# First projection of a transformer kernel: five of eight weight jobs as three products of short-fp32 parts, parameter loads on the GpSimd queue

## The reference, cut to what matters

```python
h = rms_norm(x, norm1_g[l]) * (1 + sc1) + sh1
z = h @ w_in[l]                       # 256 x 1024 by 1024 x 3896
y_fox = fox_mixer(z[..., :FOX_COLS], ...)
y_rwkv = rwkv7_mixer(z[..., FOX_COLS:], ...)

def fox_mixer(zf, qn_g, kn_g, on_g, forget_b):
    q, k, v, g, f_logit, a_k, a_v = split_cols(zf, FOX_SPLITS)
    k = a_k * shift_prev(k) + (1 - a_k) * k      # a_k, a_v: sigmoids
    v = a_v * shift_prev(v) + (1 - a_v) * v
    q = rms_norm(q, qn_g)
    k = rms_norm(k, kn_g)
    log_f = jax.nn.log_sigmoid(f_logit + forget_b)
    cum = jnp.cumsum(log_f, axis=1)
    ...                                          # attention of 8 heads of 64

def rwkv7_mixer(zr, mu, ...):
    zr = zr + mu * (shift_prev(zr) - zr)         # all 1824 columns
    r, k, v, wd, ad, gd = split_cols(zr, RWKV_SPLITS)
    ...
```

## Time and profile before

| | us |
|---|---|
| median of 3 runs | 1384.34 (1383.09 to 1384.56) |
| profiled execution, whole | 1383.96 |
| span in the profile | 1381.5 |
| PE busy | 1313.4 (95%) |
| DVE busy | 622.7 (45%) |
| ACT busy | 351.2 (25%) |
| POOL busy | 44.1 (3%) |

### The profile page before, as it was taken

The page is one execution under the profiler, slowest core; times in us unless marked ns, Lnnn a source line. Parts: engine busy times, 40 slices in busy tenths (PEclk is TensorE's granted clock), DMA queues, the critical chain, the costliest instruction groups (busy, mean ns, idle before and its releaser), DMA issues.

```text
span 1381.5 us, 19977 instructions
## 1 busy us (share of the span) xinstructions
PE 1313.4 (95%) x7904; PEld 834.0 (60%) x7904; DVE 622.7 (45%) x1174; ACT 351.2 (25%) x609; POOL 44.1 (3%) x50
## 2 busy tenths in 40 slices
PE   5999998999899999999999999899999998999997
PEld 2545546965544444544444444578778566999985
DVE  2135377567422222222222222565448743677753
ACT  0202320012122221222222121454321112344542
POOL 0014200000000000000000000300000000000000
PEclk9999999999999999999999999999889999999998
DMA  9684284049299999999999996654611131455551
GB/s 342 235 263 152 101 366 160 2 117 407 112 397 422 419 409 423 412 418 418 417 414 421 407 419 240 230 166 153 135 19 61 62 122 61 153 183 185 186 197 73
DMA packets 96072, 341.19 MB, mean 247 GB/s; under 512 B 9248, under 2 KB 42680, under 8 KB 67213
## 3 DMA queue, kind: packets, MB, share of 16 engines
q1 hardware_dynamic: 85728, 321.16, 60.6%
q10 hardware_dynamic: 8109, 12.33, 3.4%
q0 software_dynamic: 2176, 6.86, 1.5%
HBM read 333.22 MB, written 1.05 MB: 242 GB/s over the span
## 4 chain that ended last, share of the span: by engine, by line
PE 86%; DVE 7%; DMA 4%; issue 1%; ACT 1%; ACTq 0%; DVEq 0%
PE bank L1890 17%; PE bank L1364 12%; PE bank L1906 9%; PE bank L1379 6%; PE bank L1380 6%; PE bank L1381 6%; PE bank L1852 3%; PE bank L1870 2%; PE bank L1872 2%; PE bank L1853 2%; DMA small<-in_norm_g 2%; PE bank L1350 2%; PE bank L1391 2%; PE bank L2280 2%; DMA ring<-in_w_in 1%; PE bank L1978 1%
## 5 line engine op out<-in xcount | busy, mean ns | idle before, releaser
L1364 PE MATMUL bank<-ring,xT 128*128 128x512 f32 (+1 forms) x416 | 180.4, 590 | 6.2 <-DVE xT L2454 2.3
L1364 PEld LDWEIGHTS bank<-ring,xT 128*128 128x128 f32 x416 | 79.5, 194 | 94.6 <-issue 84.3
L1906 PE MATMUL bank<-dn,tmp 128*64 128x512 f32 x528 | 120.6, 598 | 0.0
L3008 DVE TENSOR_TENSOR xT<-bank,mod 128x512 fp32r<-128x512 f32 x66 | 45.7, 692 | 157.9 <-ACT mod L1114 150.6
L3001 DVE SCALAR_TENSOR_TENSOR tmp<-silu_c,rc,bank 128x256 f32<-128x256 f32 x33 | 22.6, 685 | 196.8 <-ACT silu_c L1101 191.4
L1379 PE MATMUL bank<-mod,w_high 128*128 128x256 f32 x304 | 85.1, 280 | 0.0
L1380 PE MATMUL bank<-xn,w_high 128*128 128x256 f32 x304 | 85.1, 280 | 0.0
L1381 PE MATMUL bank<-mod,ring 128*128 128x256 f32 x304 | 84.8, 279 | 0.0
L3495 DVE TENSOR_TENSOR ring<-ring,w_high 128x1024 fp32r<-128x1024 f32 x60 | 70.7, 1221 | 21.7 <-ACT w_high L1299 20.2
L1906 PEld LDWEIGHTS bank<-dn,tmp 128*64 128x64 f32 x528 | 35.0, 136 | 68.3 <-issue 68.3
L1114 ACT ACTIVATE mod<-bank 128x512 fp32r<-128x512 f32 x64 | 38.2, 597 | 133.8 <-PE bank L1906 133.8
(11 more groups left out here) (654 smaller groups left out, 2296.9 us busy)
## 6 DMA issues: line engine op xcount, KB each, us to landing
dn<-in_exp_w_down SPq DMA_DIRECT2D x66, 1024.0 KB, 10.6
ring<-in_exp_w_gate SPq DMA_DIRECT2D x34, 1024.0 KB, 9.9
ring<-in_exp_w_up SPq DMA_DIRECT2D x34, 1024.0 KB, 12.5
gu_odd<-in_exp_w_gate SPq DMA_DIRECT2D x32, 1024.0 KB, 10.3
gu_odd<-in_exp_w_up SPq DMA_DIRECT2D x32, 1024.0 KB, 12.3
ring<-in_w_ffn_in SPq DMA_DIRECT2D x22, 1024.0 KB, 5.1
ring<-in_w_in SPq DMA_DIRECT2D x7, 2048.0 KB, 11.3
ring<-in_w_in SPq DMA_DIRECT2D x14, 912.0 KB, 4.9
```

The costliest lines, as they stand in the source:

```text
L1364: mm = pe.matmul(bank[lin_bank(o)][:, 0:n], lhs(k, t), ring[:, j % RING, k * n:(k + 1) * n], start=(k == 0), stop=(k == kt - 1 and not bias))
L1906: mm = pe.matmul(bank[6 + h][CHUNKS[c], :], act_eT[:, 0, k, CHUNKS[c]], dn[:, 2 * parity + c, lo:lo + BANK], start=(k == 0), stop=(k == D_ ...
L3008: dve.tensor_tensor(y_low[:, c], bank[6 + h][:, :], y_high[:, c].bitcast(F32), ALU.subtract)\
```

## The change

- J_K, J_V, J_Q, J_R and J_KR (`SPLIT`) are computed by `split_job` as three products each: 48 matmuls instead of 16. J_LORA, J_VR and J_G stay as they are.
- ScalarE makes the high parts of the weights (`split_high`, from `ring` into the new `w_high_1`, one buffer of two halves), VectorE the low ones in place of the weights (`split_low`), in pieces of 1024 columns, four a job. The parts of `xT` are made once, in two halves (`xT_high_1` by ScalarE, `xT_low_1` by VectorE).
- A split job is loaded as two halves of 1 MB. Half 0 of a load waits for the first half of job j-2 (`in_done`), half 1 for its end. `split_high` of half 0 waits until both halves have landed and the first half of the job before is used; that of half 1 waits for the last matmul of the job before, and stands behind its two copies (`copies_beside_split`). TensorE takes half 0 for both tiles, then half 1 for both.
- The loads of `forget_b`, `fxp`, `mu`, of the ten constants and matrices, and of `rwp` and `gain` move to POOL's queue; the ten wait for the end of J_LORA, `rwp` and `gain` for the first lerp and the end of J_Q. `ada_b`'s rows stay with ScalarE.
- The shift of J_LORA moves ahead, right behind the forget gate's chain on ScalarE.
- VectorE's low parts stand between its other steps. Later counts of the shared semaphores are offset accordingly; the diff leaves these lines out, but for one.

```diff
--- before.py
+++ after.py
@@ -259,6 +259,8 @@
+with ExitStack() as before_aug:
+    w_high_1 = stack_r(before_aug, "w_high_1", [P, 2, KT // 2 * BANK])
@@ -581,14 +583,20 @@
-def job(kind, w, lo, n, kt=KT, bias=None, more=0):
+def job(kind, w, lo, n, kt=KT, bias=None, more=0, halves=False):
+    def half(h):
+        ks = slice(h * kt // 2, (h + 1) * kt // 2)
+        dst = lambda slot: ring[:, slot, 0:kt * n].rearrange("p (k n) -> p k n", k=kt)[:, ks, :]
+        return dst, A[w].rearrange("(k p) n -> p k n", p=P)[:, ks, lo:lo + n]
...
-    parts = [part(0, lo, n - more)]
+    parts = [half(0), half(1)] if halves else [part(0, lo, n - more)]
     if more:
@@ -601,9 +609,12 @@
 J_LORA, J_K, J_V, J_Q, J_R, J_KR, J_VR, J_G = range(len(IN_JOBS))
+SPLIT = (J_K, J_V, J_Q, J_R, J_KR)
 for j, (lo, n) in enumerate(IN_JOBS):
...
         job("in", "w_in", lo, n + FG, more=FG)
+    elif j in SPLIT:
+        job("in", "w_in", lo, n, halves=True)
     else:
@@ -661,6 +672,29 @@
+HALF = KT // 2 * BANK
+xT_high_1 = mod_12[:, 0:2, :].rearrange("p a (k c) -> p (a k) c", c=T * P)
+xT_low_1 = xn_low[:, :, :].rearrange("p a (k c) -> p (a k) c", c=T * P)
+def landed_of(j):
+    return sum(16 * len(jobs[i][4]) for i in range(j % RING, j + 1, RING))
+def split_piece(a, j, half, q):
+    lo = half * HALF + q * PIECE
+    return a[:, j % RING, lo:lo + PIECE]
+def high_piece(half, q):
+    return w_high_1[:, half, q * PIECE:(q + 1) * PIECE]
+def piece_no(j, half, q):
+    return 4 * SPLIT.index(j) + 2 * half + q + 1
+IN_1 = 4 * len(SPLIT)
@@ -747,6 +781,15 @@
         for j in range(first, last):
+            if j in SPLIT:
+                for h, (dst, src) in enumerate(jobs[j][4]):
+                    if j >= RING:
+                        if h == 0 and j - RING in SPLIT:
+                            sp.wait_ge(in_done, SPLIT.index(j - RING) + 1)
+                        else:
+                            sp.wait_ge(lin_mm, last_of(j - RING))
+                    sp.dma_start(dst(j % RING), src).then_inc(w_full[j % RING], 16)
+                continue
             if j >= RING:
...
@@ -907,13 +950,22 @@
     rstd(small[:, 18:20], small[:, 16:18])
-    act.wait_ge(ada_mm, 1)
-    act.dma_start(forget_b[:, :], bcast(A["fox_forget_b"])).then_inc(forget_loaded, 16)
-    for j in range(RING):
-        act.wait_ge(w_full[j], 16 * len(jobs[j][4]))
-    for i, name in enumerate(("fox_qn_g", "fox_kn_g", "fox_on_g")):
-        act.dma_start(fxp[:, i, :], bcast(A[name])).then_inc(forget_loaded, 16)
-    act.dma_start(mu[:, :], bcast(A["rw_mu"])).then_inc(mu_loaded, 16)
+    for h in range(2):
+        c = slice(h * KT // 2, (h + 1) * KT // 2)
+        act.wait_ge(h_ready, (h + 1) * KT // 2)
+        act.activation(xT_high_1[:, c, :], xT[:, c, :], ACT.Copy).then_inc(x_high_made, 1)
+    def split_high(j, half):
+        s = SPLIT.index(j)
+        if half == 0:
+            act.wait_ge(w_full[j % RING], landed_of(j))
+            if s:
+                act.wait_ge(in_done, s)
+        elif s:
+            act.wait_ge(lin_mm, last_of(SPLIT[s - 1]))
+        for q in range(2):
+            act.activation(high_piece(half, q), split_piece(ring, j, half, q), ACT.Copy).then_inc(in_high_made, 1)
@@ -935,7 +987,10 @@
-    for t in range(T):
+    split_high(J_K, 0)
+    for t in range(T):
+        if t:
+            split_high(J_K, 1)
         act.wait_ge(lin_mm, after(J_LORA, t))
@@ -948,30 +1003,25 @@
     act.activation(fs[:, 4, 0:16], fs[:, 3, 0:16], ACT.Ln, bias=1.0).then_inc(fox_ln, 1)
-    for t in range(T):
-        in_copy(J_K, t)
-    for name in CONST_1:
-        act.dma_start(cst[name][:, :], consts[name]).then_inc(par_loaded, 16)
-    act.dma_start(lora_up[0:DECAY_R, :], A["rw_decay_up"]).then_inc(par_loaded, 16)
-    act.dma_start(lora_up[DECAY_R:P, :], A["rw_iclr_up"]).then_inc(par_loaded, 16)
-    act.dma_start(gate_up[:, 0, :], A["rw_gate_up"][0:P, :]).then_inc(par_loaded, 16)
-    act.dma_start(gate_up[0:GATE_R - P, 1, :], A["rw_gate_up"][P:GATE_R, :]).then_inc(par_loaded, 16)
+    shift_group(0, J_LORA)
+    def copies_beside_split(j, following):
+        split_high(following, 0)
+        for t in range(T):
+            in_copy(j, t)
+        split_high(following, 1)
+    copies_beside_split(J_K, J_V)
     for b in range(2):
...
             .then_inc(ada_rows, 16)
-    for t in range(T):
-        in_copy(J_V, t)
+    copies_beside_split(J_V, J_Q)
     act.wait_ge(lin_evac, after(J_V, 1))
     shift_rows(kv_prev, z_fox[:, :, 512:1536], kv_shifted)
-    for i, name in enumerate(("rw_w0", "rw_a0", "rw_k_k", "rw_k_a", "rw_r_k", "rw_lnx_g", "rw_lnx_b")):
-        act.dma_start(rwp[:, i, :], bcast(A[name])).then_inc(par_loaded, 16)
-    act.dma_start(gain[:, 1, :], bcast(A["norm2_g"])).then_inc(gain_loaded[1], 16)
-    shift_group(0, J_LORA)
-    for t in range(T):
-        in_copy(J_Q, t)
-    for t in range(T):
-        in_copy(J_R, t)
+    copies_beside_split(J_Q, J_R)
+    copies_beside_split(J_R, J_KR)
     shift_group(1, J_R)
@@ -1440,15 +1490,37 @@
     keep_warm(4, 7)
+    def split_job(j):
+        full[j % RING] += 16 * len(jobs[j][4])
+        for half in range(2):
+            for t in range(T):
+                o = outputs[(j, t)]
+                if half == 0 and o >= 2:
+                    pe.wait_ge(lin_evac, o - 1)
+                for i in range(KT // 2):
+                    k = half * KT // 2 + i
+                    if t == 0 and i % 2 == 0:
+                        pe.wait_ge(in_low_made, piece_no(j, half, i // 2))
+                    mm = product(bank[lin_bank(o)][:, :],
+                                 [a[:, k, t * P:(t + 1) * P] for a in (xT_high_1, xT_low_1)],
+                                 [w_high_1[:, half, i * BANK:(i + 1) * BANK],
+                                  w_low[:, j % RING, k * BANK:(k + 1) * BANK]], k == 0, k == KT - 1)
+                if half:
+                    mm.then_inc(lin_mm, 1)
+            if half == 0:
+                mm.then_inc(in_done, 1)
     dense(J_LORA, first_lhs)
-    dense(J_K, xTk)
+    pe.wait_ge(x_low_made, 2)
+    split_job(J_K)
     pe.wait_ge(logf_ready, 1)
...
     for j in (J_V, J_Q, J_R, J_KR):
-        dense(j, xTk)
+        split_job(j)
     keep_warm(10, 2)
...
@@ -1993,7 +2065,7 @@
                 if t == 0 and i % 2 == 0:
-                    pe.wait_ge(in_low_made, (u - 2) * PIECES + i // 2 + 1)
+                    pe.wait_ge(in_low_made, IN_1 + (u - 2) * PIECES + i // 2 + 1)
                 mm = product(b, [a[:, k, t * P:(t + 1) * P] for a in (xT_high, xT_low)],
...
@@ -2343,6 +2415,20 @@
+    pool.wait_ge(ada_mm, 1)
+    pool.dma_start(forget_b[:, :], bcast(A["fox_forget_b"])).then_inc(forget_loaded, 16)
+    for j in range(RING):
+        pool.wait_ge(w_full[j], 16 * len(jobs[j][4]))
+    for i, name in enumerate(("fox_qn_g", "fox_kn_g", "fox_on_g")):
+        pool.dma_start(fxp[:, i, :], bcast(A[name])).then_inc(forget_loaded, 16)
+    pool.dma_start(mu[:, :], bcast(A["rw_mu"])).then_inc(mu_loaded, 16)
+    pool.wait_ge(lin_mm, after(J_LORA, 1))
+    for name in CONST_1:
+        pool.dma_start(cst[name][:, :], consts[name]).then_inc(par_loaded, 16)
+    pool.dma_start(lora_up[0:DECAY_R, :], A["rw_decay_up"]).then_inc(par_loaded, 16)
+    pool.dma_start(lora_up[DECAY_R:P, :], A["rw_iclr_up"]).then_inc(par_loaded, 16)
+    pool.dma_start(gate_up[:, 0, :], A["rw_gate_up"][0:P, :]).then_inc(par_loaded, 16)
+    pool.dma_start(gate_up[0:GATE_R - P, 1, :], A["rw_gate_up"][P:GATE_R, :]).then_inc(par_loaded, 16)
     pool.wait_ge(mu_loaded, 16)
@@ -2355,6 +2441,11 @@
         pool.sem_inc(lerp_done, 1)
+        if i == 0:
+            pool.wait_ge(lin_mm, after(J_Q, 1))
+            for r, name in enumerate(("rw_w0", "rw_a0", "rw_k_k", "rw_k_a", "rw_r_k", "rw_lnx_g", "rw_lnx_b")):
+                pool.dma_start(rwp[:, r, :], bcast(A[name])).then_inc(par_loaded, 16)
+            pool.dma_start(gain[:, 1, :], bcast(A["norm2_g"])).then_inc(gain_loaded[1], 16)
     pool.wait_ge(experts_copied, 1)
@@ -2453,7 +2544,22 @@
             .then_inc(h_ready, 1)
+    for h in range(2):
+        c = slice(h * KT // 2, (h + 1) * KT // 2)
+        dve.wait_ge(x_high_made, h + 1)
+        dve.tensor_tensor(xT_low_1[:, c, :], xT[:, c, :], xT_high_1[:, c, :].bitcast(F32), ALU.subtract)\
+            .then_inc(x_low_made, 1)
     link(dve.memset(kv_prev[0:1, 0, :], 0.0))
+    def split_low(j, half):
+        for q in range(2):
+            dve.wait_ge(in_high_made, piece_no(j, half, q))
+            dve.tensor_tensor(split_piece(w_low, j, half, q), split_piece(ring, j, half, q),
+                              high_piece(half, q).bitcast(F32), ALU.subtract).then_inc(in_low_made, 1)
+    split_low(J_K, 0)
+    split_low(J_K, 1)
@@ -2463,20 +2569,30 @@
     dve.tensor_tensor(fs[:, 5, 0:16], fs[:, 1, 0:16], fs[:, 4, 0:16], ALU.subtract).then_inc(logf_ready, 1)
+    split_low(J_V, 0)
     dve.wait_ge(sc_mm, SC_CUMF + 1)
...
     dve.sem_inc(sc_evac, 1)
+    split_low(J_V, 1)
```

(8 more changed lines are left out.)

14 lines of the change are left out of this document (7 added, 7 removed).

## The result

The changed kernel takes 1392.72 us (median of four runs, 1390.68 to 1393.74) beside 1384.45 us of the kernel before (1383.09 to 1384.71): ratio 1.006, interval 1.0042 to 1.0077. It is slower by 0.6%; the prediction was 1384.0 with a range to 1388.5. The profiled execution took 1392.32 us, with a span of 1390.2, 8.7 more than before.

What follows compares the result with a forecast made beforehand. TensorE bounds the kernel before, VectorE after the change. Transposes 1.2 us sooner, 0.9 back to the clock: 0.3 less than 1383.96, so 1383.6, plus 0.4 for the median: 1384.0; own range 1381 to 1387, overall range 1372.5 to 1388.5.

Steps and rivals of the forecast that it cites:

- What bounds the kernel, and the question asked: TensorE bounds the kernel up to 121.64; the question is when the transposes of `q_aug` can start, with VectorE becoming the bound.
- The products: TensorE's split jobs: 48 matmuls at 0.232 us, 11.1 us a job instead of 13.85, 13.8 us less for five.
- J_V's load: J_V's weights, asked for at 46.2, take 10.3 us and land at 56.5; TensorE waits 1.6 us, first product at 58.9.
- Rival 3: J_V's weights land late, at 59, and the clock falls: 4.2 us more than the sum, 1388.2; chance 19%.
- The rows of k and v: Shifted rows for VectorE's lerp land 5 us after ScalarE issues them, at 80.5; with 10.9 they would cost TensorE 4.5 us.
- The exclusion of VectorE and POOL: POOL's lerp instructions hold VectorE's last two groups: three cost 7.0 us, two more 4.7, moving `aug_ready` from 108.7 to 120.4.
- rival 2: Only one POOL lerp meets VectorE, J_KR's rows coming perhaps 3 us later: transposes at 115.7, 1379.3 us; chance 16%.
- Rival 1: POOL does not hold two-input VectorE instructions: transposes at 108.7, 1371 to 1377 us, likely 1374; chance 26%.
- POOL's issues: Loads moved to POOL's queue cost 0.5 us each to issue, when POOL has nothing else to do; ScalarE is rid of them.
- Sum at the transposes: Transposes start at 120.4 instead of 121.64, 1.2 us less.
- The clock behind the wait: After TensorE's 15 us wait the low clock falls on the transposes; half of 1.7 us is taken, 0.9 us.
- What is won or lost at 121.64 is won or lost at the end: The transposes' start and the end of the span move by the same amount; otherwise the prediction is wrong altogether.

Runs made afterwards that it cites:

- experiment 1: Changed kernel with POOL issuing the ten parameter loads after J_K instead of after J_LORA: 1385.96 us, ratio 1.0014 to the kernel before.
- experiment 5: Changed kernel with the ten parameter loads issued on SP's queue right behind J_V's halves: 1385.96 us, ratio 1.0008 to the kernel before.
- Experiment 8: Experiment 4 with 16 warming matmuls instead of 30 and the three `fxp` broadcasts issued with the ten after J_K: 1388.49 us, ratio 1.0026.
- experiment 10: Changed kernel with the ten loads on SP's queue behind J_V and POOL's lerp of J_R held until `aug_ready`: 1378.09 us, ratio 0.9956.
- experiment 2: Changed kernel with POOL's lerp of J_R held until `aug_ready`: 1380.58 us, ratio 0.9979 to the kernel before.
- experiment 3: Changed kernel with 56 warming matmuls instead of ten ahead of TensorE's wait for `aug_ready`: 1391.98 us.
- experiment 9: Experiment 8 with `rwp` and `gain` issued behind POOL's lerp of J_R instead of at J_Q's end: 1398.84 us, ratio 1.0102.
- experiment 12: Experiment 10 with J_KR as one fp32 job again, so four split jobs: 1383.55 us, ratio 0.9992.
- experiment 4: Changed kernel with ten loads after J_K, POOL's lerp of J_R held until `aug_ready` and 30 warming matmuls: 1383.03 us, ratio 0.9986.
- experiment 6: Changed kernel with J_R and J_KR as fp32 again, so three split jobs: 1388.02 us, ratio 1.0022 to the kernel before.
- experiment 7: Experiment 6 with the ten loads issued after J_K: 1382.16 us, ratio 0.9987 to the kernel before.
- experiment 11: Experiment 10 with `rwp` and `gain` issued behind POOL's lerp of J_R, after `aug_ready`: 1391.15 us, ratio 1.0047.

## Why the prediction was wrong, step by step

**What bounds the kernel, and the question asked:** right. The transposes' start decided more than half of it, and VectorE is what they wait for.

**The products:** right. 0.232 us forecast, 0.228 measured; J_K ended at 57.3 as said. The cover of the split held as well: TensorE waited 0.6 and 0.4 us for low parts, both where VectorE's lerp of k and v stands ahead of them.

**J_V's load: the step that failed.** I took 10.3 us, the time of J_Q's load beside the same ten; it took 16.57 us from the issue of its second half. Neither row that I had was the case at hand. J_Q had only the ten beside it. J_V's own 8.9 us were not "beside little else", as the prediction says: `fxp` and `mu` (1.7 MB) were issued just ahead of it in the kernel before as well. ScalarE's timeline there, and `mu`'s time to landing, which gives 49.8:

```profile
40.74 0.34 ACTq L915 DMA_DIRECT2D fxp<-in_fox_qn_g  x1
...
42.07 0.45 ACTq L916 DMA_DIRECT2D mu<-in_rw_mu  x1
```

```profile
mu<-in_rw_mu ACTq DMA_DIRECT2D x1, 912.0 KB, 7.7
```

In the changed kernel J_V meets both: the ten, which moved up by one job, and `fxp` and `mu`, which were issued 1.3 to 1.6 us later on POOL's queue and landed at 52.0. So J_V took 7.7 us more than before. Experiment 1 takes the ten away and gives 5.2 of them back, experiment 5 puts them behind J_V and gives as much. The other 2.5 us were not taken apart: `mu` landed 2.2 us later than before, and J_LORA's shift, which the change moved ahead, was in flight from 51.6 on. Experiment 8 shows only that J_V is not waited for without `fxp`. The row that was nearest was J_R's 15.60, beside 2.3 MB of broadcasts and the rows of k and v, and I had read it as the far end. TensorE's first product came at 65.9 instead of 58.9, and the low clock cost J_V another 2.2 us (66 to 79.2, 13.3 us instead of 11.1). Rival 3 named place and mechanism and was sized too small: it stopped at a landing of 59.

**The rows of k and v:** 5 us after the last issue forecast, 9.4 measured. That made only 1.3 us against J_V's end, because they were issued sooner behind it. They came at 91.0 instead of 80.5. From there VectorE ran almost without a pause; the second norm was ready at 111.2 instead of 101.8, 9.4 us later, since the forecast had 1.1 us to spare there. In experiments 1 and 10 the rows moved by 3.9 and 5.2 us, and the second norm by the same.

**The exclusion of VectorE and POOL:** right, and shown by experiment 2: taken away, 7.9 us at the transposes. Its size was 8.1 us instead of the 11.7 forecast: the first lerp cost 6.3 us and not 7.0, and J_KR's rows came (123.94) when one short instruction was left, so three instructions met, then one, and not three and two. That is near rival 2's outcome, but not by its reason: the rows came 10.6 us behind J_KR's end, as in the forecast, and not 3 us later. Rival 1 falls: two-input instructions of 0.69 us took 2.7. The Trainium skill (SBUF — State Buffer, "Who interferes with whom") calls the shared pair an exclusive lock; this case's rows agree, and show that each side waits for the other's whole instruction. Two inputs are not needed: the copy of line 2610 and line 2613, both 128x8 with one input in SBUF, took 2.19 and 1.97 us instead of 0.17, as had line 2497 in the earlier trace rows; copies out of PSUM were not held (experiment 2).

**POOL's issues:** no sign that they starve. The ten went out 0.53 us apart (46.64 to 51.41 for nine steps). The Trainium skill (SBUF — State Buffer, "SBUF: two separate sides") warns that loads issued by GpSimd wait while VectorE runs in a mode that uses both ports, as an fp32 copy within SBUF does. Nothing of the kind held these: VectorE's subtractions for J_K ran until 47.3, beside the first two issues, and the ten landed 5.5 to 8.8 us after their issue. It was J_V on SP's queue that was late.

**Sum at the transposes:** 120.4 + 9.4 - 3.7 = 126.1, measured 126.4. The whole distance from forecast to measured time, 8.7 us, is these 6.0 us, 0.8 for the clock in the transposes, 2.7 for the clock near 220, less 0.8 elsewhere. In the 6.0, J_V's late start and the clock behind it are 9.2 us, and the smaller price of the exclusion takes 3.7 back.

**The clock behind the wait:** 0.9 us taken, 1.7 measured; with warming (experiment 3) 1.4 came back in the trace, and in the median 0.7, which can't be told from nothing.

**"What is won or lost at 121.64 is won or lost at the end":** only roughly, and the prediction had named this as the sign of being wrong altogether. The transposes' start moved by 4.8 us, the end of the span by 8.7. The largest piece between them is the second low stretch of the clock near 220, 2.7 us, behind the same wait of 2.3 us as before. It is not shown that the change causes it. In the profiled executions this wait is followed by the lower level in the changed kernel and in experiments 1, 2, 3, 5, 8, 9 and 12 (granted 0.50 to 0.71 over the next 4 us), and by 1.00 in the kernel before and in experiments 4, 6, 7, 10 and 11. A stretch ahead of the change's first wait differs in the same way: J_LORA took 10.3 to 10.4 us in the kernel before, in the changed one and in experiments 1 to 4, 6 and 10 (granted clock 0.55 to 0.60 over 36 to 40 us), and 8.6 us in 5, 7, 8, 9, 11 and 12 (1.00), though 10 and 11 issue the same work up to there. So two executions can differ by 1.7 and 2.7 us without an edit as the reason. This may be a part of why the runs of one kernel spread over 4 us and more; why the clock falls in one and not in the other is open.

**Where the gain of the products went.** By the measured 0.228 us five jobs need 14.5 us less (five times 13.85 - 10.94), and TensorE then came to its loads before they had landed. Experiment 8 shows it best: one load helped, the next late by more. Experiments 6 and 12 show that TensorE can't simply take work back from VectorE, since whole loads of 2 MB came 3.0 and 3.5 us late there. What paid was order in the queues and keeping POOL away; experiment 10 has both.

## What to carry to other kernels

When loads move to another queue or to an earlier moment, list all bytes that are in flight beside the next load that the bound engine waits for, those already under way included, and price that load by the row whose company is the largest. Ten small loads behind the critical one in its own queue left it alone here and made TensorE wait 0.8 to 2.4 us for the next load in that queue; issued by GpSimd beside it they cost it 5.2. Before VectorE becomes the bound, look at what GpSimd does in the same microseconds, and hold it back if it has time. And see what each wait asks for before a load is moved: a wait for more loads than its user needs turned a harmless delay of `rwp` into 10.9 us.

## What the runs showed of the hardware that was not expected

- Ten loads (1.4 MB) issued by POOL while two halves of 1 MB were in flight on SP's queue held these until 63.4; issued by SP behind them in nearly the same moments they let them land at 57.3 to 57.8 (experiments 5, 10, 11 and 12), no later than with ten loads issued 11 us later (58.1, experiment 1).
- A half of 1 MB of a weight load took between 5.1 and 23.8 us from issue to landing in this stretch, over these kernels, depending on what stood beside it. At a DMA share of 1.05 the engines moved 335 GB/s over 50 to 60 us of the changed kernel, and 386 at the same share in the earlier trace rows.
- VectorE and GpSimd took turns instruction by instruction, and VectorE's one-input instructions of 128x8 on SBUF were held as its two-input ones were (2.19 instead of 0.17 us).
- Behind the same wait of 2.3 us, and over the same fp32 work at 36 to 40 us, the granted clock was at the lower level for a while in some executions and at 1.00 in others.
- Five kernels in which J_V came sooner or VectorE had less to do (4, 6, 7, 8 and 12) ended in a wait of 2.6 to 15.5 us for a later load.
